# The routed experts' down product in three fp32r products of high and low parts, in a two-layer trunk kernel

## The reference, cut to what matters

```python
gu = jnp.einsum('nd,edf->nef', t, lp['w_exp_gu'])                     # 32 experts, 1024 -> 2 x 256
a = jax.nn.silu(gu[..., :EXPERT_FF]) * gu[..., EXPERT_FF:]
a = (a * combine[..., None].astype(a.dtype)).reshape(-1, N_EXPERTS * EXPERT_FF)
routed = a @ lp['w_exp_down'].reshape(N_EXPERTS * EXPERT_FF, D_MODEL)  # 256 -> 1024 per expert
sgu = t @ lp['w_sh_gu']
shared = (jax.nn.silu(sgu[:, :SHARED_FF]) * sgu[:, SHARED_FF:]) @ lp['w_sh_down']
return (routed + shared).reshape(B, T, D)
```

## Time and profile before

| what | us |
|---|---|
| median of 3 executions | 2116.08 (2113.89 to 2118.29) |
| the profiled execution | 2117.09 |
| its span | 2115.5 |
| TensorE busy | 1874.5 (89%) |
| VectorE busy | 1140.9 (54%) |
| ScalarE busy | 886.2 (42%) |
| expert loop, layer 1 and layer 2 | some 320 each |

### The profile page before, as it was taken

One profiled execution on the slowest core, in us unless ns is written; L12 is line 12 of the kernel. 1 busy time (PEld: TensorE's weight loads), 2 busy tenths in 40 slices (PEclk: granted clock), 3 DMA queues, 4 the chain that ended last, 5 costly groups with the idle time before them and its releaser, 6 DMA issues. The chain is left out here.

```text
span 2115.5 us, 26897 instructions
## 1 busy us (share of the span) xinstructions
PE 1874.5 (89%) x8784; PEld 1322.4 (63%) x8784; DVE 1140.9 (54%) x1670; ACT 886.2 (42%) x1510; POOL 425.4 (20%) x485
## 2 busy tenths in 40 slices
PE   6998998999978999999169989989999779999990
PEld 3886666888764666555038866568887646655550
DVE  2345557444545666665523455575444556666655
ACT  3342346433342555554133423464333525555541
POOL 2003312400004222332120042114000042333320
PEclk9999998999999999999589999989999999999995
DMA  8433271343434899998374423704334349999973
GB/s 297 155 122 114 88 252 27 111 138 120 139 143 148 327 346 344 340 344 293 128 271 143 137 96 118 242 7 130 120 123 156 147 150 326 350 345 341 343 265 155
DMA packets 114892, 419.97 MB, mean 199 GB/s; under 512 B 18992, under 2 KB 26768, under 8 KB 82544
## 3 DMA queue, kind: packets, MB, share of 16 engines
q1 hardware_dynamic: 90368, 372.28, 50.1%
q0 software_dynamic: 20928, 40.06, 6.2%
q10 hardware_dynamic: 3504, 6.43, 0.8%
HBM read 411.77 MB, written 32.18 MB: 210 GB/s over the span
## 5 line engine op out<-in xcount | busy, mean ns | idle before, releaser
L1381 DVE TENSOR_TENSOR W_split<-W,W_split 128x2048 fp32r<-128x2048 f32 (+3 forms) x96 | 224.7, 2343 | 407.5 <-ACT W_split L1022 407.5
L1890 PE MATMUL psum<-W_split,qT_split 128*128 128x512 f32 (+3 forms) x1536 | 405.3, 376 | 8.3 <-ACT hT L991 8.1
L1022 ACT ACTIVATE W_split<-W 128x2048 fp32r<-128x2048 f32 (+3 forms) x96 | 175.9, 1838 | 406.1 <-PE psum L1890 370.5
L1890 PEld LDWEIGHTS psum<-W_split,qT_split 128*128 128x128 f32 x1536 | 284.9, 190 | 57.8 <-ACT hT L991 8.7
L1890 PE MATMUL psum<-W_split,scratch_split 128*128 128x512 f32 x864 | 275.4, 391 | 0.6 <-DVE hT_split L1376 0.6
L1830 PE MATMUL psum<-W,zf 128*96 128x512 f32 (+1 forms) x560 | 257.0, 602 | 14.9 <-ACT zf L1282 11.8
L1779 DVE TENSOR_TENSOR W_split<-W,qT_split 128x2048 fp32r<-128x2048 f32 x64 | 146.7, 2292 | 207.0 <-ACT qT_split L1254 207.0
L1254 ACT ACTIVATE qT_split<-W 128x2048 fp32r<-128x2048 f32 x64 | 122.6, 1916 | 235.1 <-DMA W<-in_w_exp_gu 141.7
L1890 PE MATMUL psum<-W_split,hT_split 128*128 128x512 f32 x576 | 210.1, 392 | 5.8 <-DVE scratch_split L1579 5.8
L2135 PE MATMUL psum<-qT_split,hT_split 128*96 128x512 f32 x512 | 199.5, 451 | 6.3 <-issue 6.3
L2135 PE MATMUL psum<-W_split,hT_split 128*96 128x512 f32 x512 | 203.1, 397 | 0.0
(11 more groups left out here) (317 smaller groups left out, 2652.4 us busy)
## 6 DMA issues: line engine op xcount, KB each, us to landing
W<-in_w_exp_gu SPq DMA_DIRECT2D x128, 1024.0 KB, 10.4
W<-in_w_exp_down SPq DMA_DIRECT2D x64, 1024.0 KB, 9.4
W<-in_w_in SPq DMA_DIRECT2D x60, 1024.0 KB, 5.1
W<-in_w_mod SPq DMA_DIRECT2D x48, 1024.0 KB, 4.9
W<-in_w_br SPq DMA_DIRECT2D x16, 1024.0 KB, 5.1
W<-y_rows SPq DMA_DIRECT2D x6, 2048.0 KB, 13.1
W<-in_w_out SPq DMA_DIRECT2D x8, 1024.0 KB, 5.0
kT<-mod_rows POOLq DMA_DIRECT2D x8, 512.0 KB, 5.3
```

The source lines that it names most:

```text
L1022: nc.scalar.activation(high(j), piece(SPLITS[j]), ACT.Copy).then_inc(S["high_ready"], 1)
L1381: V.tensor_tensor(piece(SPLITS[j], Wr), piece(SPLITS[j]), high(j).bitcast(F32), ALU.subtract).then_inc(S["low_ready"], 1)
L1890: ins = nc.tensor.matmul(bank(job, piece_size(key)[1]), act_part[:, k0 + k, t * P:(t + 1) * P], w_part[:, k, :], start=first and (k, i) == ...
```

## The change

The down product of the routed experts is made like gate-up: weights and turned activations are each split in a high and a low fp32r part, and three products are added in PSUM: high activations x high weights, low x high, high x low. The shared expert's down product stays as it is. In the loop:

- TensorE: `down_split` in place of `down`, twelve products a tile. It waits for the low part of the activations (`aT`, now taken by VectorE) and of the down weights (`dn_low`) and no longer for the landing itself.
- ScalarE: the copy of the turned activations now writes their high part; y1's copy comes to ScalarE, behind y0's; behind that the high part of the next tile's down weights (`down_weights_high`, 128x2048) into `down_high`, one buffer.
- VectorE: `product` comes first, then the low part of the turned activations (`product_low`), then first half, rows and second half of gate-up, then the low part of the next tile's down weights (`down_weights_low`, in place in `W`). y1's copy is gone.
- The new buffers lie in `zf`, over the mixture rows, so the first conversion of down weights waits until these are written out (`rows_out`). GpSimd's and SyncE's work is the same.

```diff
-STEP = (("gu", "dve"), ("aT", "act"), ("xt0", "dve"), ("xt1", "dve"), ("y0", "act"), ("y1", "dve"))
+STEP = (("gu", "dve"), ("aT", "dve"), ("xt0", "dve"), ("xt1", "dve"), ("y0", "act"), ("y1", "act"))
...
-        aT = zf[:, 7168:7168 + 4 * CAP].rearrange("p (s f n) -> p s f n", s=2, f=2)
+        aT_split = [zfr[:, at:at + 4 * CAP].rearrange("p (s f n) -> p s f n", s=2, f=2) for at in (5120, 5120 + 4 * CAP)]
+        down_high = zfr[:, 3072:5120].rearrange("p (k n) -> p k n", k=2)
...
+                    def down_weights_high(s):
+                        nc.scalar.activation(down_high, expert_dn(s), ACT.Copy).then_inc(S["dn_high"], 1)
+
...
+                    act.wait_ge(S["rows_out"], 16 * T)
+                    act.wait_ge(S["dn_landed0"], 16)
+                    down_weights_high(0)
...
-                            nc.scalar.activation(aT[:, e].rearrange("p f n -> p (f n)"), psum[:, BANK_AT, 0:2 * CAP],
-                                                 ACT.Copy).then_inc(S["act_emptied"], 1)
+                            nc.scalar.activation(aT_split[0][:, e].rearrange("p f n -> p (f n)"), psum[:, BANK_AT, 0:2 * CAP],
+                                                 ACT.Copy).then_inc(S["aT_high"], 1)
...
                             nc.scalar.activation(yrow[0:CAP, e, 0:C], psum[0:CAP, BANK_Y, :], ACT.Copy).then_inc(S["act_emptied"], 1)
+                            act.wait_ge(*job_filled(turn, e, "y1", LESS["y"][e] if last else 0))
+                            nc.scalar.activation(yrow[0:CAP, e, C:], psum[0:CAP, BANK_Y + 1, :], ACT.Copy).then_inc(S["act_emptied"], 1)
+                            if not (last and e == 1):
+                                act.wait_ge(S[f"dn_landed{1 - e}"], turn * 16 + 32)
+                                down_weights_high(1 - e)
...
+                    def down_weights_low(s, tile):
+                        dve.wait_ge(S["dn_high"], AHEAD + tile + 1)
+                        V.tensor_tensor(expert_dn(s, Wr), expert_dn(s), down_high.bitcast(F32), ALU.subtract).then_inc(S["dn_low"], 1)
+
+                    def product_low(s, tile):
+                        high_part, low_part = (v[:, s].rearrange("p f n -> p (f n)") for v in (aT_split[0].bitcast(F32), aT_split[1]))
+                        dve.wait_ge(S["aT_high"], AHEAD + tile + 1)
+                        V.tensor_tensor(low_part, psum[:, BANK_AT, 0:2 * CAP], high_part, ALU.subtract).then_inc(S["dve_emptied"], 1)
...
                             tile = turn * 2 + e
+                            if not (last and e == 1):
+                                product(BANK_GU + 1 - e, 1 - e, tile + T + 2)
+                            product_low(e, tile)
                             if not last:
                                 weights_low(e, 0, tile * 2 + 4)
-                            if not (last and e == 1):
-                                product(BANK_GU + 1 - e, 1 - e, tile + T + 2)
-                            if not last:
                                 rows_low(e, tile * 2 + 4)
                                 weights_low(e, 1, tile * 2 + 4)
-                            dve.wait_ge(*job_filled(turn, e, "y1", LESS["y"][e] if last else 0))
-                            dve.wait_ge(S[f"y_written{e}"], turn * 16 + 16)
-                            V.tensor_copy(yrow[0:CAP, e, C:], psum[0:CAP, BANK_Y + 1, :]).then_inc(S["dve_emptied"], 1)
+                            if not (last and e == 1):
+                                down_weights_low(1 - e, tile + 1)
...
+                    def down_split(dst, s, c):
+                        parts = [(aT_split[a], (down_high, expert_dn(s, Wr))[b]) for a, b in ((0, 0), (1, 0), (0, 1))]
+                        multiply(psum[0:CAP, dst, :], [(act_part[:, s, f, :], w_part[:, f, c * C:(c + 1) * C]) for act_part, w_part in parts for f in range(2)]
+                                 ).then_inc(S["psum_filled"], 1)
...
-                            pe.wait_ge(*job_emptied(turn, e, "aT"))
-                            pe.wait_ge(S[f"dn_landed{e}"], turn * 16 + 16 * (e + 1))
+                            pe.wait_ge(*job_emptied(turn, e, "aT", LESS["dve"][e] if last else 0))
+                            pe.wait_ge(S["dn_low"], AHEAD + turn * 2 + e + 1)
                             pe.wait_ge(*job_emptied(*before, "y0"))
-                            down(BANK_Y, aT[:, e], e, 0, CAP)
-                            pe.wait_ge(*job_emptied(*before, "y1", gone))
-                            down(BANK_Y + 1, aT[:, e], e, 1, CAP)
+                            down_split(BANK_Y, e, 0)
+                            pe.wait_ge(*job_emptied(*before, "y1"))
+                            down_split(BANK_Y + 1, e, 1)
```

More of the change, by code:

```diff
@@ L367, in trunk @@
         hT, hTr = sb_twice("hT", KD * T * P)
-        zf = sb("zf", 13824)
+        zf, zfr = sb_twice("zf", 13824)
         W, Wr = sb_twice("W", SLOTS * SLOT)
@@ L419, in trunk @@
         names += ["dec_scaled", "mixture_rows", "post_root", "pre_root", "halves_used", "high_ready", "low_ready", "h_split", "oT_high", "mgT_high",
-                  "gu_half_used", "gu_high", "gu_low", "x_high"]
+                  "gu_half_used", "gu_high", "gu_low", "x_high", "dn_high", "dn_low", "aT_high"]
         landed_names = [f"piece_landed{i}" for i in range(RAW)] + [f"gu_landed{s}{h}" for s in range(2) for h in range(2)] + ["dn_landed0", "dn_landed1"]
@@ L547, in trunk, with expert_dn @@
         gate_up_high = [t[:, 0:SLOT // 2].rearrange("p (k n) -> p k n", k=KD // 2) for t in (qTr, scratchr)]
-        def expert_dn(s):
-            return W[:, 2 * SLOT + s * SLOT // 2:2 * SLOT + (s + 1) * SLOT // 2].rearrange("p (k n) -> p k n", k=2)
+        def expert_dn(s, tensor=W):
+            return tensor[:, 2 * SLOT + s * SLOT // 2:2 * SLOT + (s + 1) * SLOT // 2].rearrange("p (k n) -> p k n", k=2)
         def landed(key):
@@ L594, in previous @@
             return (turn, 0) if e == 1 else (turn - 1, 1)
-        LESS = {"aT": (0, 3), "y": (2, 5), "dve": (2, 5)}
+        LESS = {"aT": (0, 3), "y": (2, 5), "dve": (0, 3)}
         def turns_of(eng):
@@ L705, in _ @@
                     sp.sem_inc(S["gu_low"], AHEAD)
+                    for name in ("aT_high", "dn_high", "dn_low"):
+                        sp.sem_inc(S[name], AHEAD)
                     for i, key in enumerate(PIECES):
@@ L911, in of_tile, with write_rows @@
                         return table[0:CAP, tile:tile + 1, word] if isinstance(tile, int) else table[0:CAP, bass.ds(tile, 1), word]
-                    def write_rows(turn, e, less=0):
+                    def write_rows(turn, e):
                         pool.wait_ge(*job_emptied(turn, e, "y0"))
                         pool.sem_inc(S["gathers"], 1)
-                        pool.wait_ge(*job_emptied(turn, e, "y1", less))
+                        pool.wait_ge(*job_emptied(turn, e, "y1"))
                         pool.sem_inc(S["gathers"], 1)
@@ L949, in _ @@
                     for e in range(2):
-                        write_rows(turns - 1, e, LESS["dve"][e])
+                        write_rows(turns - 1, e)
                     pool.wait_ge(S["cache_out"], 16 * 8)
@@ L1784, in _ @@
                         rows_low(i, 2 * i)
+                    down_weights_low(0, 0)
                     weights_low(1, 0, 2)
@@ L2155, in steps @@
                             before = previous(turn, e)
-                            gone = (2 if last and e == 1 else 0)
                             if not (last and e == 1):
```

## The result

The changed kernel takes 2126.92 us (median, 2120.42 to 2134.55), the kernel before, measured beside it, 2116.08: a ratio of 1.0052 with a 95% interval of 1.0038 to 1.0066. That is 10.8 us slower where 9 were forecast. The execution profiled took 2127.13 us (span 2125.4).

A forecast was written before the change was run, and what follows sets the result against it. Two limits 3% apart were taken to bound the kernel: TensorE at 10.04 us a tile, and the loads. 2117.09 + 4.4 (loops) + 0 (load-paced tiles) + 4.5 (layer ends) = 2126.0, less 1.0 to the median: 2125; range 2118 to 2133.

The forecast's parts named there:

- TensorE's saving: Expert loop's down product: TensorE alone would save 0.67 us a tile, 43 us over 64 tiles; none expected to arrive.
- The ring: Expert loop: circle from silu through VectorE's operations to gate-up and the next silu, 10.17 us a tile against 10.04.
- Tiles paced by loads cost nothing: Expert loop: the 26 tiles limited by loads cost nothing, at most +3 us, since bytes and issue order stay.
- The loops together: Both layers' expert loops: 34 tiles paced by TensorE at +0.13 us each, +4.4 us, ends +1 and +7.5.
- the new path: Expert loop, behind a late landing: way to the next gate-up after the change, 6.29 us against 6.17 before.
- rival 3: Expert loop: down weights land too late, flights past 11.4 us making ScalarE wait; +18 us, 2143; chance 0.12.
- The end of the layer: Each layer's last turn: second down waits for the single buffer; 15.3 us against 12.90, +2.2 a layer, +4.5 for two.
- the term of the twelve matmuls: Layer's end: the last down's twelve matmuls, at lower clock after some 5 us of idleness, take 4.67 us.
- The hidden work: Expert loop: added conversions stay hidden, ScalarE 8.1 and VectorE 8.4 of 10 us busy; at most 1 us a layer.
- the cheap ends: Layer ends: the low case of the +4.5 us, without clock loss, +1 us.
- rival (1): Loop: short hand-overs and loads making up time cancel the cost; about 2118, 2112 with cheap layer ends; chance 0.18.
- rival (2): Loop: TensorE's saving comes through with VectorE's rows early; about 2111, 2105 with a mild end; chance 0.06.

The follow-up runs named there:

- e5: Changed kernel with the loop's down-weight loads cut to 128 KB of each 1 MB; 2120.16 us, ratio 1.0017.
- e1: Changed kernel with two buffers for the high down weights, the second tile's converted ahead of the first's output copies in the last turn; 2115.74 us, ratio 0.9994.
- e2: Changed kernel with the low part of gate-up's first half made in two pieces, one ahead of VectorE's product, one behind the low activations; 2127.43 us, ratio 1.0056.
- e7: Changed kernel with VectorE's first half in two pieces and the down loads cut to 128 KB of each 1 MB; 2104.78 us, ratio 0.9948.
- e4: Kernel before the change with VectorE's two post-norm gain operations moved from behind the expert loop to its start; 2111.3 us, ratio 0.9968.
- e8: Changed kernel with VectorE's old order: low part of gate-up's first half ahead of the product and the low activations; 2165.36 us, ratio 1.0223.
- e9: Changed kernel with two buffers for the high down weights, the first half in two pieces and the post-norm gains moved ahead of the loop; 2113.15 us, ratio 0.9989.

## Why the prediction was right, and where its sizes were off

- **TensorE's saving.** A down product of 2.77 and a tail was forecast, 3.02 it is; TensorE is busy 1856.4 us instead of 1874.5 over the whole kernel. That none of the saving arrives was right; that TensorE would be busy some 40 us less was not, the difference is 18. Over the 53 tiles of the two stretches the down product's 0.65 makes 34.5, but gate-up's 0.26 of waiting for rows stands inside its matmuls and is counted as busy (13.8), and the slow matmuls of the two long tiles take 1.55 and 1.39 more: 17.8, where the stretches show 8.55 + 8.52.
- **The ring.** From the silu's start to the rows' end 4.25 was summed and 4.22 measured; the tile 10.17 and 10.20. TensorE's waits are 0.50 ahead of down in most tiles, 0.59 in the mean (46.7 us over the kernel in the page's row, less 5.04 at each layer's end, by 62), and 5.81 - 5.55 = 0.26 in gate-up, where 0.5 and 0.3 were given:

```profile
L1853 PE MATMUL psum<-zf_split 128*96 128x512 f32 x512 | 149.7, 416 | 46.7 <-DVE zf_split L1802 46.7
```

- **Tiles paced by loads cost nothing.** Right in the mean. Without the loads' limit the change costs 14.6 us from the loops' first load to `y_rows`, both layers together; with it 10.7. The 3.9 hidden are what 24 tiles at 0.16 (10.20 against 10.04) make; the prediction had 26 at nothing.
- **The loops together.** +4.4 was forecast and some 5.6 measured. Which tiles the 1.2 left over lie in isn't shown. Each layer has one long tile, 13.06 us at 920.1 and 12.65 at 1957.5. Chain of waits of the latter:

```profile
1947.11 11.58 DMA W<-in_w_exp_gu
...
1960.62 0.36 ACT zf L1289
...
1961.91 4.57 PE psum L1853 x12
```

  A first half lands late, ScalarE has its conversion ahead of the silu, TensorE waits 1.66 us, and the twelve matmuls behind it take 4.57 us instead of 3.02. Behind a late landing the prediction had the new path 0.12 us longer than the old one (6.29 against 6.17); it had not priced the slow matmuls, and the late landings to which it gave a chance were those of down weights (rival 3). No flight of these in the loops is over 11.4 us, its bound for no cost. In `e5` the long tiles are gone. Why a particular load is late wasn't found. That the loops came out within 1.2 us is partly luck: these are single executions, and in that of `e1`, whose loop is the same, late landings make the way from layer 1's first silu to its last 327.0 us instead of 320.4.
- **The end of the layer.** 15.3 was forecast and 15.74 measured in layer 2: the term of the twelve matmuls was mis-sized, 4.67 against 5.26, at a mean granted clock of 0.53. The term holds to some 0.7 us only, since behind the same pause of 5.04 they take 4.95 in layer 1, 4.40 in `e2` and 5.37 in `e7`. Index copy 0.18 and a landing of 3.32 are as taken (0.18 and 3.4); the first down after the silu took 4.37 (4.30). The pause of some 5 us was 5.04.
- **The hidden work.** ScalarE's and VectorE's added conversions stay beside TensorE's work. ScalarE waits for down weights only three times in 26 tiles of layer 2, 1.3 us in all.
- **Two side sums.** With the cheap ends at +1, rival (1) adds up to 2116.08 + 1 - 4 + 1 = 2114 and not 2112, and rival (2) to 2107 and not 2105, so the chance below 2111.9 in (1) has no sum behind it. The measured time lies far from both.

## What to carry to other kernels

An operation split into cheaper products is paid where its operands are made: sum the ring that runs through the converting engine, in its queue's order, before counting what the multiplying engine saves. One buffer that is enough in the steady loop can be the dearest thing at the loop's end, where no other work lies between two uses; it costs the conversion, and the pause can cost clock behind it. When two limits lie close, measure each with the other removed, since a gain against one (two pieces: 15.4 us with cheap loads) can vanish in the other (none with full loads).

## What the runs showed of the hardware

**GpSimd's copies and issues are held up while VectorE subtracts out of SBUF.** In the loop after the change, timelines of GpSimd:

```profile
1858.18 2.30 POOL L931 COPY vm<-vm 96x1 uint32 x1 [0.25 <-PE psum L2152]
1861.35 3.08 POOL L934 DMA_INDIRECT zf<-token_rows,vm  x1 [0.86 <-ACT zf L1300]
```

and of VectorE:

```profile
1858.16 2.28 DVE L1793 TENSOR_TENSOR W_split<-W,qT_split 128x2048 fp32r<-128x2048 f32 x1
...
1861.29 2.28 DVE L1793 TENSOR_TENSOR W_split<-W,scratch_split 128x2048 fp32r<-128x2048 f32 x1
```

The index copy (0.18 when alone) ends at 1860.48, 0.04 behind VectorE's operation, and the issue of the gather (0.98 when alone, 2.75 in the mean of the kernel after, 1.14 before) ends at 1864.43, 0.86 behind the other. Nobody waits for either in the loop; at the layer's end the path runs through them, and that is what `e4` gained. The Trainium skill, SBUF — State Buffer, section Who interferes with whom, states the first (a VectorE instruction with two SBUF inputs blocks a GpSimd one that reads SBUF) and infers that writing descriptors isn't blocked; here the issue of a gather and of a scatter is held up too (`e4`: 3.31 against 4.61 to the landing). As both read their row numbers from `vm` in SBUF, the runs don't show whether that reading waits or the writing of descriptors.

**The clock can fall after a short pause, and its length alone doesn't decide.** Granted clock by stretch (column behind POOL's) in the kernel after: the last twelve matmuls of layer 2, the twelve of the long tile, and the 1.66 us pause ahead of these:

```profile
2073.48:2078.74 5.26, 5.24 (x12) 3.15 (x12) 4.26 (x2) 0.59 (x1) 0.00 (x0) 0.53 0.00 0
...
1961.91:1966.48 4.57, 4.57 (x13) 3.12 (x14) 4.57 (x4) 2.54 (x3) 0.59 (x1) 0.63 0.85 341
...
1960.25:1961.91 1.66, 0.01 (x1) 0.00 (x1) 0.91 (x3) 1.66 (x5) 0.58 (x2) 1.00 1.01 415
```

A mean of 0.53 or 0.63 is a mix of TensorE's two levels, 1.2 GHz (0.50) and 2.4 (1.00). In `e8` TensorE pauses for 1.46 us ahead of each down in the loop and the twelve take 3.02; here a pause of 1.66 was followed by a fall. In `e9` a pause of the same length, behind the same gate-up and transposes, was followed by none (timeline of TensorE, then the stretch):

```profile
1997.58 0.69 PE L1867 MATMUL psum<-zf_split 128*96 128x512 f32 x2 [1.66 <-DVE zf_split L1813]
...
1997.60:2000.60 3.00, 3.00 (x13) 2.15 (x14) 2.85 (x4) 2.40 (x2) 1.68 (x1) 1.00 1.00 411
```

What does decide isn't shown. Where the clock falls, a late load costs more than its lateness: in the long tile 1.66 us of waiting, where 0.50 is usual, and 1.55 of slow matmuls.
